# Building the scaled key rows of the expert gates on GpSimd, VectorE and ScalarE

## The reference, cut to what matters

```
idx = i1 * PEER_N_KEYS + i2                 # i1, i2: first and second key, 0..127
g = jax.nn.softmax(best, axis=-1)
act = gelu(einsum('ckd,cd->ck', u_tab[ic], xc))
out = einsum('ck,ckd->cd', gc * act, v_tab[ic])
```

## Time and profile before

| | |
|---|---|
| median of 3 executions | 3473.45 us (3460.08 to 3475.53) |
| the profiled execution's own time | 3467.66 us |
| its span | 3466.1 us |
| mean granted TensorE clock | 0.956 |
| gates of the first expert layer | about 1551.8 to 1667 us of the span |
| gates of the second expert layer | about 2704.3 to 2819.6 us of the span |

### The profile page before, as it was taken

One profiled execution on the slowest core, in us unless ns is written; L12 is line 12 of the kernel. 1 busy time (PEld: TensorE's weight loads), 2 busy tenths in 40 slices (PEclk: granted clock), 3 DMA queues, 4 the chain that ended last, 5 costly groups with the idle time before them and its releaser, 6 DMA issues.

```text
span 3466.1 us, 50181 instructions
## 1 busy us (share of the span) xinstructions
PE 3180.4 (92%) x18944; PEld 2700.9 (78%) x18944; DVE 2029.0 (59%) x4174; ACT 1648.6 (48%) x3566; POOL 111.2 (3%) x176
## 2 busy tenths in 40 slices
PE   7998999997899878996899999988799679999999
PEld 4745677776799767985789999978698568999998
DVE  2233433335665665689666666657569876666665
ACT  2244322223655335319655555543441875555554
POOL 0022000000200020000000000001100000000000
PEclk9989999998999878999999999989699999999999
DMA  5501444432155313440355655543144025555654
GB/s 212 182 1 68 158 170 169 157 106 80 50 185 178 136 62 95 155 135 1 128 186 187 187 185 188 187 158 111 36 166 152 31 72 185 187 184 188 188 183 152
DMA packets 135055, 479.85 MB, mean 138 GB/s; under 512 B 15520, under 2 KB 17440, under 8 KB 134048
## 3 DMA queue, kind: packets, MB, share of 16 engines
q1 hardware_dynamic: 132944, 471.26, 41.6%
q10 hardware_dynamic: 1872, 5.38, 0.4%
HBM read 475.53 MB, written 1.05 MB: 137 GB/s over the span
## 4 chain that ended last, share of the span: by engine, by line
PE 87%; DVE 6%; issue 4%; ACT 3%; DMA 1%; ACTq 0%; DVEq 0%; SPq 0%
PE psum L763 15%; PE psum L765 14%; PE psum L764 14%; PE psum L2577 7%; PE psum L2579 7%; PE psum L2578 7%; PE psum L2498 7%; PE psum L2422 4%; PE psum L853 2%; PE psum L1112 2%; PE psum L354 1%; PE psum L613 1%; PE psum L1122 1%; PE psum L627 1%; DVE a_scaled L728 1%
## 5 line engine op out<-in xcount | busy, mean ns | idle before, releaser
L248 DVE TENSOR_TENSOR w_lo<-raw,w_hi 128x512 fp32r<-128x512 f32 x1440 | 971.3, 691 | 788.2 <-ACT w_hi L239 760.0
L239 ACT ACTIVATE w_hi<-raw 128x512 fp32r<-128x512 f32 x1440 | 875.1, 625 | 823.2 <-PE psum L765 450.1
L763 PE MATMUL psum<-x_hi,w_hi 128*128 128x256 f32 x2032 | 581.6, 286 | 3.6 <-DVE x_lo L679 3.6
L765 PE MATMUL psum<-x_hi,w_lo 128*128 128x256 f32 x2032 | 580.1, 285 | 0.0
L764 PE MATMUL psum<-x_lo,w_hi 128*128 128x256 f32 x2032 | 576.9, 284 | 0.0
L2577 PE MATMUL psum<-w_hi,wt_hi 128*128 128x512 f32 x1024 | 407.5, 398 | 6.5 <-DVE wt_lo L2635 6.5
L2579 PE MATMUL psum<-w_hi,wt_lo 128*128 128x512 f32 x1024 | 406.0, 396 | 0.0
L2578 PE MATMUL psum<-w_lo,wt_hi 128*128 128x512 f32 x1024 | 405.2, 396 | 0.0
L763 PEld LDWEIGHTS psum<-x_hi,w_hi 128*128 128x128 f32 x2032 | 389.1, 191 | 12.1 <-issue 4.0
L764 PEld LDWEIGHTS psum<-x_lo,w_hi 128*128 128x128 f32 x2032 | 391.9, 193 | 8.0
L765 PEld LDWEIGHTS psum<-x_hi,w_lo 128*128 128x128 f32 x2032 | 387.5, 191 | 0.0
(11 more groups left out here) (312 smaller groups left out, 4432.3 us busy)
## 6 DMA issues: line engine op xcount, KB each, us to landing
raw<-in_v SPq DMA_DIRECT2D x256, 512.0 KB, 4.4
raw<-in_u SPq DMA_DIRECT2D x190, 512.0 KB, 3.4
raw<-in_mod_w SPq DMA_DIRECT2D x96, 512.0 KB, 4.4
raw<-in_w_gate_up SPq DMA_DIRECT2D x88, 512.0 KB, 4.9
u_raw<-in_u SPq DMA_DIRECT2D x66, 512.0 KB, 3.4
raw<-in_w_in SPq DMA_DIRECT2D x40, 512.0 KB, 3.5
raw<-in_w_down SPq DMA_DIRECT2D x32, 512.0 KB, 3.5
raw<-in_w_peer SPq DMA_DIRECT2D x32, 512.0 KB, 4.2
```

The lines of the kernel that those rows point to most:

```text
L239: self.nc.scalar.activation(self.hi[:, m % 4, :], self.half(m), ACT.Copy).then_inc(self.rounded[m % 4], 1)
L248: self.nc.vector.tensor_tensor(self.lo[:, m % 4, :], self.half(m), self.hi[:, m % 4, :], ALU.subtract).then_inc(self.ready[m % 4], 1)
L763: pe.matmul(out[:, 0:width], hi[:, w], x_hi, start=(c == 0), stop=False)
L765: mm = pe.matmul(out[:, 0:width], lo[:, w], x_hi, start=False, stop=(c == total - 1))
```

## The change

The second-key rows are no longer compared in one step and scaled in another. One GpSimd instruction per token makes (iota == key) * weight for tokens 0, 1 and 2 of each group. The row of token 3 is made by DVE in even groups (one instruction) and by ACT in odd groups (two instructions: the distance |key - iota|, then relu(weight - 2 * distance), which leaves the weight at distance zero and zero elsewhere). DVE's comparison with the second keys and ACT's four scalings go. The row of numbers that DVE reads is now a copy in PSUM bank 4, made once per layer by a matmul of the identity with `iota`; GpSimd and ACT still read `iota` in SBUF. DVE's comparison with the first keys stays, with the PSUM row as its first input. Bank 4 becomes free for `Experts` when the last comparison has read it.

```diff
+        self.numbers = k.bank[4].use(read=self.GROUPS)
-        self.first_made = k.named("first_key_rows").take(self.GROUPS)
-        self.scaled = k.named("rows_scaled").take(self.GROUPS)
+        self.by_vector = k.named("fourth_row_by_vector").take(self.GROUPS // 2)
+        self.by_scalar = k.named("fourth_row_by_scalar").take(self.GROUPS // 2)
...
     def tensor(self):
-            pe.wait_ge(*self.first_made.after(g + 1))
-            pe.wait_ge(*self.scaled.after(g + 1))
+            pe.wait_ge(*self.numbers.emptied(g + 1))
+            pe.wait_ge(*self.second_made.after(g + 1))
+            pe.wait_ge(*(self.by_scalar if g % 2 else self.by_vector).after(g // 2 + 1))
...
+    def tensor_numbers(self):
+        pe = self.k.nc.tensor
+        pe.wait_ge(*self.numbers.free())
+        pe.matmul(self.numbers.tensor[:, 0:P], self.k.ident, self.iota[:], start=True,
+                  stop=True).then_inc(self.numbers.written.sem, 1)
+
+    def gpsimd(self):
+        pool = self.k.nc.gpsimd
+        hold(pool, self.routed)
+        for g in range(self.GROUPS):
+            if g >= 4:
+                pool.wait_ge(*self.uses[g - 4].full())
+            for t in range(3):
+                n = 4 * g + t
+                m = pool.tensor_scalar(self.rows(g, t), self.iota[:], self.slots[:, 2, n:n + 1],
+                                       self.slots[:, 0, n:n + 1], ALU.is_equal, ALU.mult)
+            m.then_inc(self.second_made.sem, 1)
...
     def make(self, g):
-        dve.tensor_tensor(self.second[g % 4], row_no.rearrange("p (c k) n -> p c k n", c=2),
-                          keys[1].rearrange("p (c k) n -> p c k n", c=2), ALU.is_equal).then_inc(self.second_made.sem, 1)
-        dve.tensor_tensor(self.first[:, g % 4], row_no, keys[0], ALU.is_equal).then_inc(self.first_made.sem, 1)
+        dve.tensor_tensor(self.first[:, g % 4], row.unsqueeze(1).to_broadcast([P, 4, P]),
+                          self.slots[:, 1, 4 * g:4 * g + 4].unsqueeze(2).to_broadcast([P, 4, P]),
+                          ALU.is_equal).then_inc(self.numbers.read.sem, 1)
+        if g % 2 == 0:
+            n = 4 * g + 3
+            dve.tensor_scalar(self.rows(g, 3), row, self.slots[:, 2, n:n + 1], self.slots[:, 0, n:n + 1], ALU.is_equal,
+                              ALU.mult).then_inc(self.by_vector.sem, 1)
...
     def scalar(self):
+        hold(self.k.nc.scalar, self.routed)
         for g in range(self.GROUPS + 2):
             if g >= 2:
                 self.move_late(g - 2)
-            if g < self.GROUPS:
-                self.scale(g)
+            if g < self.GROUPS and g % 2 == 1:
+                self.fourth_row(g)
+
+    def fourth_row(self, g):
+        k, act, row, n = self.k, self.k.nc.scalar, self.rows(g, 3), 4 * g + 3
+        if g >= 4:
+            act.wait_ge(*self.uses[g - 4].full())
+        away = k.sstep(act.activation(row, self.iota[:], ACT.Abs, bias=self.slots[:, 2, n:n + 1], scale=-1.0))
+        act.wait_ge(*away)
+        act.activation(row, row, ACT.Relu, bias=self.slots[:, 0, n:n + 1],
+                       scale=-2.0).then_inc(self.by_scalar.sem, 1)
...
         self.scored.tensor()
+        self.gate.tensor_numbers()
         self.route.tensor()
         self.gate.tensor()
...
-        for layer in self.layers[0::2]:
+        for layer in self.layers:
             layer.gpsimd()
```

More of the change, by code:

```diff
@@ L2424, in tensor @@
             m.then_inc(use.written.sem, 1)
+    def tensor_numbers(self):
[14 more added lines that the diff above has]
+            m.then_inc(self.second_made.sem, 1)
     def vector(self):
         hold(self.k.nc.vector, self.routed)
+        self.k.nc.vector.wait_ge(*self.numbers.full())
         for g in range(self.GROUPS + 2):
@@ L2434, in make @@
     def make(self, g):
[L2435 to L2438, removed]
+        dve, row = self.k.nc.vector, self.numbers.tensor[:, 0:P]
         if g >= 4:
             dve.wait_ge(*self.uses[g - 4].full())
-        dve.tensor_tensor(self.second[g % 4], row_no.rearrange("p (c k) n -> p c k n", c=2),
-                          keys[1].rearrange("p (c k) n -> p c k n", c=2), ALU.is_equal).then_inc(self.second_made.sem, 1)
-        dve.tensor_tensor(self.first[:, g % 4], row_no, keys[0], ALU.is_equal).then_inc(self.first_made.sem, 1)
+        dve.tensor_tensor(self.first[:, g % 4], row.unsqueeze(1).to_broadcast([P, 4, P]),
[5 more added lines that the diff above has]
+                              ALU.mult).then_inc(self.by_vector.sem, 1)
     def weigh_early(self, g):
@@ L2694, in tensor, with gpsimd @@
         self.experts.tensor()
+    def gpsimd(self):
+        self.gate.gpsimd()
     def scalar(self):
```

## The result

The changed kernel took 3543.70 us (median of 4 executions, 3541.61 to 3547.77) against 3472.11 for the kernel before: a ratio of 1.0215, 95% interval 1.0192 to 1.0237. It is 71.6 us slower, where 48 us faster was forecast. That it is slower is clear of the noise; whether by a full 2% is left open by the interval.

The account below looks back on a forecast made before the run. ACT's throughput was taken to bound the gates at 1.756 us per group; (1.756 - 1.37) x 62 x 2 = 48 us off 3467.66 gave 3420, or 3425 off the median, the forecast. Range: 3404 to 3460.

Parts of the forecast that it names:

- GpSimd's part: Three GpSimd rows per group in the gates, 0.40 us each taken: 1.2 to 1.3 us per group.
- the upper bound: Highest price for a GpSimd row in the gates, from a two-input 64x256 row: 0.735 us, 2.2 for three.
- the ring: Gates' waits from move through Abs, Relu and matmuls to move: 1.37 us per group taken, 1.28 to 1.44; chance 0.57.
- the second, GpSimd's row dearer than 0.585: Rival in the gates: GpSimd's row above 0.585 us makes the kernel slower, 55 us lost at 0.735; chance 0.10.
- a third of the second: Upper third of the case that POOL decides the gates' period, up to 1.75 us per group; case's chance 0.23.
- half of the fourth: Half of the case that DVE and GpSimd block each other in the gates, 3456 or 3499; case's chance 0.06.
- the last: Case of some wait that no other case names, leaving the time about the same; chance 0.02.
- the sum: Gates of both layers: (1.756 - 1.37) x 62 x 2 = 48 us gained.
- ACT's and DVE's parts: Work per group in the gates: ACT 0.97 us, DVE 1.1 us, neither setting the period.
- Shutting out: Rival: DVE and GpSimd block each other in the gates, period 1.62 (3456) or 1.96 (3499); chance 0.06.
- Table loads: Rival: Abs or Relu needs table loads in the gates, 1.28 us each, 3 us or 82 us per layer; chance 0.02.
- Cover and ends: Numbers' matmul hidden in PE's 3.47 us route wait; start effects of about 1 us twice cancel, end stays.

Follow-up runs that it names:

- e1: Changed kernel with GpSimd's rows multiplying by the second key and the weight instead of comparing (gates not the reference's): 3431.98 us.
- e3: Changed kernel with GpSimd's rows multiplying by the key and constant 1.0, no comparison or weight (gates not the reference's): 3430.71 us.
- e6: Changed kernel with GpSimd making two rows of each group, VectorE the third and ScalarE the fourth: 3443.59 us, ratio 0.9932 to the kernel before.
- e8: Changed kernel, GpSimd two rows per group (one in every fourth), VectorE rest of three, ScalarE's fourth row ahead of group g-2's move: 3421.44 us, ratio 0.9865.
- e10: From e8, no rows on GpSimd: VectorE three in even groups, two in odd; ScalarE one and two: 3462.82 us, ratio 0.9987.
- e4: Changed kernel with VectorE reading the row of numbers from SBUF instead of the PSUM copy: 3601.54 us.
- e11: From e8, with VectorE reading the row of numbers from SBUF: 3474.73 us, ratio 1.0016 to the kernel before.
- e9: Changed kernel with GpSimd's rows cut to their first 64 elements: 3455.84 us.
- e2: Changed kernel with GpSimd's rows comparing with the second key but multiplying by constant 1.0 instead of the weight: 3513.81 us.

## Why the prediction was wrong

**The step that failed is GpSimd's part, and in it one term.** It took 0.40 us for a row, "near the one-input rows since this too reads a single tensor", and 0.735 as the upper bound. The row measured 0.777, above the bound, so that three rows take 2.33 us: GpSimd's throughput and not the ring's 1.37 sets the period. What was right: the plain row at 128 elements (0.34 worked out, 0.346 measured) and that the second pointer costs something (0.085). What was wrong was the choice between the ends: nearness went by how many tensors are read, and the price hung on the operation, which doubles the plain row (0.346 more, and 0.085 for the pointer). The two estimates that the prediction worked out from cycles per element, 0.42 and 0.51, were too low as well. The kernel before had no comparison on POOL, so the trace could not show it; the bound from another kind of instruction (a TENSOR_TENSOR of 64x256) was no bound for this one.

**The rival that happened** is the second, GpSimd's row dearer than 0.585. Its formula holds with the measured row: (2.33 - 1.756) x 124 = 71 us lost, against 71.6 measured. It had a chance of 0.10. The chances do not quite follow from the cases either: a third of the second, half of the fourth and the last come to 0.13 for no difference if the second is spread evenly, where 0.08 is stated.

**The ring was right as a mechanism** once GpSimd is quick enough (e1, e3): 1.42 per group where 1.34 to 1.44 was worked out and 1.37 taken. The parts that were off: from Relu's end to the matmul 0.25 and not 0.10, Relu 0.40 and not 0.375. With rows at 0.431, near the price that I took, e1 came out at 3432, 43.5 below the kernel before beside it; the sum had said 48. With the row at 0.777 this part could not show in the time of the changed kernel.

**ACT's and DVE's parts** were right but for small sizes. In the changed kernel Abs is 0.366 long, Relu 0.402 (0.375 each had been worked out), DVE's comparison from PSUM 0.684 and its fourth row 0.402, just above the 0.28 to 0.38 worked out. The throughputs measured since foretold which engine fills up in e6, e8 and e10.

**Shutting out** did not happen, since every VectorE instruction there has a tensor in PSUM, but it was only one edit away: e4 and e11 show its price. The forecast for such a case, all of the comparison's 0.60 per group, was too much; 0.40 to 0.45 was measured.

**Table loads** did not happen. ScalarE loads tables 27 times in either kernel, at the same lines, and e1's ring has no room for a load of 1.28. ScalarE: Activation LUTs of the Trainium skill (Table sets) has both functions in every set, and the trace agrees.

**Cover and ends.** The numbers' matmul took 0.38 us, at 1552.80 of the kernel after, while PE waited for the route. The end of the gates is as before: 3.27 us of PE's idle time ahead of the experts in both. No stage outside the gates is shown to have changed.

## What to carry to other kernels

Price an instruction on GpSimd by its operation: here a comparison cost as much again as the whole plain instruction, and a bound from a row of another operation did not hold. Once the prices were measured, dividing the rows in proportion turned 2% slower into 1.35% faster with the same parts, and the windows say when the division is right (every engine that shares the work full or nearly so, as in e8). When no engine is full, look for a ring of waits through an engine's program order; here exchanging two calls opened it. If GpSimd and VectorE work side by side, keep one of the two tensors of VectorE's comparison in PSUM: here that was worth 53 us (e11 against e8).

## What the runs showed that I had not expected

In the gates PE is not the bound, yet its granted clock is lower in the kernels whose groups come further apart. One group's matmuls last 1.13 us where the granted clock is 1.00 (2.4 GHz) and 2.05 at half of it (1.2 GHz). At a period of 1.55 (e6), 1.67 (e9) and 1.756 us per group (the kernel before) the windows of the middle 40 us show 1.00; at 2.08 (e2) 0.87; at 2.33 (the changed kernel) 0.68; at 2.73 (e4) 0.50. In e11, at 1.80, it was 0.91. These are means over 40 us, in which the clock changes between its two levels; what makes it change was not tested. The window of e4:

```profile
1600.00:1640.00 40.00, 29.70 (x117) 25.71 (x117) 17.15 (x36) 15.81 (x29) 40.00 (x45) 0.50 0.00 1
```

In e2, the changed kernel and e4 it cost nothing, since 2.05 still fits into the period; in e11 it does not fit into 1.80, but POOL's rows ran through without a wait there too. PE's busy time rises by it: 29.54 us of 40 in the changed kernel with 137 records, more than the 25.98 with 184 before. By busy time alone PE looks more loaded where it did less.
